# A hybrid decoder step on one core: row maxima turned by one matmul per group onto up to four rows of the query operand

## The chip, the cores and the metric

The kernel runs on one core of one Trainium2 chip. The metric is the device time of one execution in microseconds. A core has a matrix engine (TensorE; PE in the profile, PEld for its weight loads), VectorE (DVE), ScalarE (ACT), GpSimd (POOL) and SyncE (SP), which here issues most DMAs. Each engine runs its own queue of instructions in order and waits on semaphores that the others count up. A matmul writes to one of 8 PSUM banks; all other tiles lie in SBUF, in 128 partitions.

## What is computed

One inference step of a decoder trunk with a short-convolution layer and a forgetting-attention layer, for a prompt of 1040 tokens (1024 and 16 learned ones) and for 32 sample tokens over a paged cache. Only the attention of the prompt heads bears on the change:

```python
def forget_attention(q, k, v, c_q, c_k, q_pos, k_pos):
    s = jnp.einsum('nqhd,nkhd->nhqk', q, k, preferred_element_type=jnp.float32) * (HEAD_DIM ** -0.5)
    s = s + (jnp.transpose(c_q, (0, 2, 1))[:, :, :, None] - jnp.transpose(c_k, (0, 2, 1))[:, :, None, :])
    causal = k_pos[None, :] <= q_pos[:, None]
    s = jnp.where(causal[None, None], s, NEG_INF)
    p = jax.nn.softmax(s, axis=-1)
    return jnp.einsum('nhqk,nkhd->nqhd', p.astype(v.dtype), v)
```

There are 16 heads of 64 values. The softmax needs the largest logit of each query (its row maximum), which is subtracted before the exponential.

## The kernel before

The trunk runs through stages: token loads and norms, convolution mixer, a first MLP, keys and values, queries, the attention of the prompt heads, the output projection together with the sample tokens' attention, a second MLP. The change lies in the prompt heads, some 271 us of the 2548.5, and in head 0's maxima, which are found among the query units ahead of them.

**Operands.** For head h the query operand QA (`q_hi_ext` in the trace) and the key operand CK (`k_hi_ext`) are [128, 1040] tiles, in three sets that take turns (SETS). Rows 0 to 63 hold the head's values, rows 64 (HD) and on hold extra terms of the dot product: 1 in QA against c in CK (rows 65 and 66), and in row 64 the maximum of the query with a minus in QA against 1 in CK. While the maxima are found, row 64 of QA holds zeros, put there by a DMA of `load_head` (L1576), which is issued up to two heads ahead. Logits come out keys by queries, so the maximum of a query has to lie along a row of QA.

**Maxima of the next head.** While head h is weighed, `max_logits` and `reduce_max` run for head h + 1, in sixteen uses u (USES) of a ring of two banks (RING): TensorE writes logits, queries by keys, VectorE reduces them. The maxima of a tile of 128 queries come out as a column of `NMR` (`row_max`). They are turned in three groups (SHIFTS): A is tiles 0 to 3 (16, 128, 128 and 128 queries), B tiles 4 to 6, C tiles 7 and 8. Per group TensorE multiplies each column with the identity (L1109), one matmul with a single column of weights per tile, side by side into one bank row; ScalarE copies that row with scale -1 into row 64 of QA (`keep_shift`, L1161) and counts `nm_kept` up. Before a bank is used again, `ring_wait` waits for its reduction or for `nm_kept`; the banks of A (u = 9), B (u = 11), C (u = 15) and then u = 1 of the next head follow each other in the same bank.

**The order of the loop.** A head is split into 8 groups g of pairs of key tile and query chunk, t = 8h + g. TensorE runs `logits(t + 2)`, then `weigh_values(t)` with the uses of the next head between its matmuls: A at g = 4, B at g = 5, C at g = 0 of its own head. ScalarE runs `exp_logits(t)`, which are two exponentials (L1214 in full precision, L1219 rounded, which counts `h_done`) and for g = 7 two small ones more (L1216, L1221); then `keep_shift` for A behind g = 5, for B behind g = 6, for C behind g = 1; then `keep_chunk` (L1292), a copy of the weighed values, for the group before last or the one before that. VectorE forms the low part of the probabilities (`probs_lo`, L1231) from both exponentials. The logits have two pairs of banks, so `logits(t + 2)` waits for `h_done` of t. The logits of the next head's first group are called logits(8) below, of its second logits(9), counted on from the head in hand; they wait for group 6 and group 7.

```python
                for i in SHIFTS[x]:
                    q, rows = max_rows(i)
                    mm = pe.matmul(PS[0:1, bank, q - first:q - first + rows], NMR[:, hh, i:i + 1], IDR[:, 0:rows],
                                   start=True, stop=True)
...
            act.activation(QA[h % SETS][HD:HD + 1, q0:q1], PS[0:1, bank_of(h, u), 0:q1 - q0], ACT.Copy, scale=-1.0)\
               .then_inc(nm_kept, 1)
```

Of the kernel before, what the change touches and what calls it, by code (L numbers as in the profile page):

```python
# [23 lines left out]
F32 = mybir.dt.float32  # L24
# [3 lines left out]
ACT = mybir.ActivationFunctionType  # L28
# [175 lines left out]
RING = 2  # L204
HI_RING = 3
SETS = 3


def max_rows(i):

    return (0, TAIL) if i == 0 else (TAIL + P * (i - 1), P)
# [8 lines left out]
def trunk(nc, a, out):  # L220

    ctx = ExitStack()
    with ctx:
# [852 lines left out]
        def bank_of(h, u):  # L1076

            return (4 if h else 6) + u % RING

        def reds_through(h, u):  # L1080

            return N_RED * h + sum(REDS[:u + 1])

        def ring_wait(h, u):

            h0, u0 = (h, u - RING) if u >= RING else (h - 1, u - RING + NUSE)
            if h0 < 0:
                return
            if USES[u0] in SHIFTS:
                pe.wait_ge(nm_kept, N_SH * h0 + "ABC".index(USES[u0]) + 1)  # L1090
            else:
                pe.wait_ge(red_done, reds_through(h0, u0))

        def max_logits(h, u):

            _, hh = head(h)
            x, bank = USES[u], bank_of(h, u)
            qa, ck = QA[h % SETS], CK[h % SETS]
            if u == 0:
                pe.wait_ge(h_loaded[h % SETS], 64 * (h // SETS + 1))  # L1100
            ring_wait(h, u)
            if u == NORM_USE + RING and NORM_HEAD < h <= NORM_HEAD + G:
                pe.wait_ge(aux_read, AX_Q + 3 * (KC - 1) + h - NORM_HEAD)
            if x in SHIFTS:
                pe.wait_ge(nm_ready, N_SH * h + "ABC".index(x) + 1)
                first = max_rows(SHIFTS[x][0])[0]
                for i in SHIFTS[x]:
                    q, rows = max_rows(i)
                    mm = pe.matmul(PS[0:1, bank, q - first:q - first + rows], NMR[:, hh, i:i + 1], IDR[:, 0:rows],  # L1109
                                   start=True, stop=True)  # L1110
            elif x == "M":
                for j, i in enumerate(FIRST_KEYS):
                    q, rows = max_rows(i)
                    pe.matmul(PS[:, bank, TAIL * j:TAIL * (j + 1)], qa[:, q:q + rows], ck[:, 0:TAIL],
                              start=True, stop=True)
                to = PS[0:TAIL, bank, P:P + TAIL]
                pe.matmul(to, qa[:, 0:TAIL], ck[:, 0:TAIL], start=True, stop=False)
                mm = pe.matmul(to, IDR[:, 0:TAIL], MASK[:, 0:TAIL], start=False, stop=True)
            else:
                i, a, b = x  # L1120
                q, rows = max_rows(i)
                mm = pe.matmul(PS[:, bank, 0:b - a], qa[:, q:q + rows], ck[:, a:b], start=True, stop=True)  # L1122
            mm.then_inc(mx_done, 1)
# [32 lines left out]
        def keep_shift(h, x):  # L1156

            u = USES.index(x)
            q0, q1 = max_rows(SHIFTS[x][0])[0], sum(max_rows(SHIFTS[x][-1]))
            act.wait_ge(mx_done, NUSE * h + u + 1)  # L1160
            act.activation(QA[h % SETS][HD:HD + 1, q0:q1], PS[0:1, bank_of(h, u), 0:q1 - q0], ACT.Copy, scale=-1.0)\  # L1161
               .then_inc(nm_kept, 1)

        def ops_done(t):

# [6 lines left out]
        def logits(t):  # L1172

            h, g = divmod(t, NG)
            if h == HEADS:
                return
            _, hh = head(h)
            qa, ck = QA[h % SETS], CK[h % SETS]
            if g == 0:
                pe.wait_ge(x_loaded[hh], 64 * (h // 2 + 1))  # L1180
            if g == 0 or CHUNK_OF[g] != CHUNK_OF[g - 1]:
                pe.wait_ge(nm_kept, N_SH * h + CHUNK_OF[g] + 1)
            ge(pe, h_done, ops_done(t - 2))
            for c, j, q0, w, keys, bank, col in GROUPS[g]:
                diagonal, paired = q0 == P * j, (g, j) in PAIRED or (g, j + 1) in PAIRED
                b, k = 2 * (t % 2) + bank, slice(P * j, P * j + keys)
                mm = pe.matmul(PS[0:keys, b, col:col + w], ck[:, k], qa[:, q0:q0 + w], start=(g, j) not in PAIRED,  # L1187
                               stop=False)
                mm = pe.matmul(PS[0:keys, b, col:col + w], DK[hh][:, k], QB[hh][:, q0:q0 + w], start=False,  # L1189
                               stop=not diagonal)  # L1190
                if (g, j) in PAIRED:
                    to = PS[:, b, 0:2 * PAIRED[g, j]].rearrange("p (a k) -> p a k", a=2)[:, :, 0:P]
                    mm = pe.matmul(to, MASK[:, :], twice(IDR[:, :]), start=False, stop=True)
                elif diagonal and not paired:
                    mm = pe.matmul(PS[0:keys, b, col:col + keys], MASK[:, 0:keys], IDR[:, 0:keys], start=False,
                                   stop=True)
            mm.then_inc(st_done, 1)
# [359 lines left out]
        def attention_loaders(stage_out):  # L1557
# [11 lines left out]
            def load_head(h):  # L1569

                n, rows = h % SETS, slice(HD * h, HD * h + HD)
                ge(sp, st_done, NG * (h - SETS + 1))
                for to, src in ((QA[n][OWN], qh_rows), (CK[n][OWN], kh_rows)):
                    sp.dma_start(to.bitcast(F32), src[rows]).then_inc(h_loaded[n], 16)
                sp.dma_start(CK[n][HD + 1:HD + 3].bitcast(F32), c_rows[h]).then_inc(h_loaded[n], 16)
                sp.dma_start(QA[n][HD:HD + 1].bitcast(F32), CK[n][HD + 3:HD + 4].bitcast(F32)).then_inc(h_loaded[n], 16)  # L1576

            def load_cross(h):

# [105 lines left out]
        def extend(n):  # L1685

            pool.memset(CK[n][EXT].bitcast(F32), 0.0).then_inc(ext_ready, 1)
            pool.wait_ge(ext_ready, 4 * n + 1)
            pool.memset(QA[n][EXT].bitcast(F32), 0.0).then_inc(ext_ready, 1)
            pool.wait_ge(ext_ready, 4 * n + 2)  # L1690
            pool.memset(CK[n][HD:HD + 1].bitcast(F32), 1.0).then_inc(ext_ready, 1)
            pool.wait_ge(ext_ready, 4 * n + 3)
            pool.memset(QA[n][HD:HD + 3].bitcast(F32), 1.0).then_inc(ext_ready, 1)
            pool.wait_ge(ext_ready, 4 * n + 4)
# [341 lines left out]
        def attention_tensor():  # L2036
            first_max(KC - 1)
            pe.wait_ge(unit_read, U_O)
            logits(1)
            pe.wait_ge(nm_kept, N_SH)  # L2040
            for t in range(NG * HEADS):
                h, g = divmod(t, NG)
                if h == HEADS - 1 and g in (2, 4):
                    past_turn(g - 2)
                    past_turn(g - 1)
                if t == 5:
                    pe.wait_ge(v_zero, 8)
                logits(t + 2)
                weigh_values(t, uses_of(h, g))


            for u in range(KC):
                unit(U_O + u, hi=HH, lo=HL, ready=o_ready if u == 0 else None,
                     mid={k: decode_step(KC * u + k) for k in range(KC)}, groups=(0, 1), bank=lambda s, g: 2 * s + g)
# [21 lines left out]
        def past_turn(g):  # L2076

            if g == 0:
                pe.wait_ge(lp_loaded, 16 * DB * NPAGE)
                pe.wait_ge(red_done, N_RED * HEADS)  # L2080
                pe.wait_ge(nm_kept, N_SH * HEADS)
            ge(pe, past_kept, g - 1)
            for x in range(4):
                mm = pe.transpose(PS[0:NH, 4 + g % 2, P * x:P * x + P], LPG[:, 4 * g + x], ident[:, :])
            mm.then_inc(past_done, 1)
# [1064 lines left out]
        def _(tensor):  # L3150
# [182 lines left out]
            for n in range(1, KC - 1):  # L3333
                sums, mid = head_sums(U_Q, n % 2, ax(AX_Q + 3 * n, 0, 0), KC + n), {}
                for k in range(len(FIRST_USES[n])):
                    def first(n=n, k=k):
                        first_max(n, k)
                    mid[2 + k] = first

                def norm(n=n, f=sums[6]):  # L3340
                    if FIRST_USES[n]:
                        pe.wait_ge(red_done, reds_through(0, FIRST_USES[n][-1]))
                        pe.wait_ge(nm_kept, sum(USES[u] in SHIFTS for u in range(FIRST_USES[n][-1] + 1)))
                    f()

                def end(n=n, f=sums[7]):
                    f()
                    if n == KC - 2:
                        first_logits()
                unit(U_Q + n + 1, mid={**mid, 6: norm, 7: end})  # L3350
# [30 lines left out]
```

## Time and profile before

| | us |
|---|---|
| median of 3 runs | 2550.76 (2548.99 to 2550.79) |
| the profiled execution's own time | 2550.68 |
| its span, first to last instruction | 2548.5 |
| TensorE busy (PE) | 2518.2, 99% |
| VectorE busy | 1819.5, 71% |
| ScalarE busy | 1050.1, 41% |

"Busy" is the time in which an engine had an instruction of its own in execution; the span's own shares are means over stages that differ. The granted TensorE clock is full through the stage of the heads. In the timelines a row gives the start in us from the span's start, the duration in us, engine, line of the code, operation, output<-input, shapes and how many instructions in a row were put together; behind it in brackets the time that the engine stood idle before and what ended it. A matmul's duration counts until its last result is written, so consecutive ones overlap; how fast they follow each other is read from their starts. In the grouped rows "a, b" is the busy time in us and the mean of one in ns.

### The profile page before, as it was taken

What the parts mean: (1) busy time and instruction counts of PE and PEld (TensorE: products, weight loads), DVE (VectorE), ACT (ScalarE), POOL (GpSimd) and SP (SyncE); (2) the same over time, 40 slices, a digit from 0 to 9 for tenths busy, and PEclk for the clock granted to TensorE, in tenths of its full rate; (3) what the DMA queues carried; (4) which work ended last, traced back from release to release, by engine and by line L of the source; (5) the groups of instructions that cost most, each with busy time, mean ns of one, the idle gap of its engine ahead of it and who ended that gap; (6) DMA issues with size and microseconds to landing.
All of it is one profiled execution on the core that took longest, in us unless ns stands there. A gap on an engine that the chain in (4) does not pass through costs nothing.

```text
span 2548.5 us, 45902 instructions
## 1 busy us (share of the span) xinstructions
PE 2518.2 (99%) x18300; PEld 2468.4 (97%) x18300; DVE 1819.5 (71%) x2462; ACT 1050.1 (41%) x1510; POOL 23.9 (1%) x48
## 2 busy tenths in 40 slices
PE   8999999999999999999999999999999999999998
PEld 8999999999999999999999999988899999999998
DVE  6434437666688998954345898877696666899986
ACT  4111124333333323365245777765553333333233
POOL 0000000000000000000000100000000000000000
PEclk9999999999999999999999999999999999999999
DMA  4111111333353322025424566634323333533112
GB/s 126 45 41 49 41 43 43 121 101 101 101 199 102 124 72 79 16 85 161 118 70 144 139 145 168 148 120 151 97 84 101 101 101 102 186 136 124 63 52 69
DMA packets 249038, 259.42 MB, mean 102 GB/s; under 512 B 18144, under 2 KB 184192, under 8 KB 248898
## 3 DMA queue, kind: packets, MB, share of 16 engines
q1 hardware_dynamic: 229638, 248.37, 31.3%
q10 hardware_dynamic: 19260, 9.09, 1.3%
q8 instruction: 99, 1.62, 0.3%
q14 instruction: 41, 0.34, 0.0%
HBM read 193.86 MB, written 63.42 MB: 101 GB/s over the span
## 4 chain that ended last, share of the span: by engine, by line
PE 92%; DVE 3%; ACT 2%; issue 1%; ACTq 0%; DMA 0%; SPq 0%; DVEq 0%
PE ps L596 28%; PE ps L808 25%; PE ps L863 24%; PE ps L828 2%; PE ps L1272 2%; PE ps L1122 1%; PE ps L1187 1%; PE ps L1273 1%; PE ps L1274 1%; PE ps L1189 1%; PE ps L710 1%; PE ps L647 1%; PE ps L1320 0%; DVE w_lo L580 0%; PE ps L1109 0%
## 5 line engine op out<-in xcount | busy, mean ns | idle before, releaser
L863 PE MATMUL ps<-h_op,w_op 128*128 128x268 f32 x4912 | 614.2, 286 | 0.2
L863 PEld LDWEIGHTS ps<-h_op,w_op 128*128 128x128 f32 x4912 | 609.5, 188 | 0.7 <-DVE w_op L903 0.6
L596 PE MATMUL ps<-x_hi,w_hi 128*128 128x358 f32 x1248 | 279.8, 330 | 2.8 <-DVE w_lo L580 1.6
L596 PE MATMUL ps<-x_hi,w_lo 128*128 128x358 f32 x1248 | 275.5, 327 | 0.0
L596 PE MATMUL ps<-x_lo,w_hi 128*128 128x358 f32 x1248 | 275.0, 326 | 0.0
L580 DVE TENSOR_TENSOR w_lo<-w_raw,w_hi 128x1024 fp32r<-128x1024 f32 x76 | 92.9, 1222 | 250.9 <-ACT w_hi L572 250.9
L874 ACT ACTIVATE w_op<-w_op_f 128x2048 fp32r<-128x2048 f32 (+1 forms) x54 | 97.6, 1808 | 381.9 <-PE ps L863 361.5
L596 PEld LDWEIGHTS ps<-x_hi,w_hi 128*128 128x128 f32 x1248 | 213.4, 189 | 6.6 <-DVE w_lo L580 2.4
L596 PEld LDWEIGHTS ps<-x_lo,w_hi 128*128 128x128 f32 x1248 | 215.8, 189 | 0.0
L596 PEld LDWEIGHTS ps<-x_hi,w_lo 128*128 128x128 f32 x1248 | 215.6, 189 | 0.0
L1060 DVE TENSOR_TENSOR t<-ps,t 128x536 f32<-128x536 f32 x180 | 128.8, 715 | 120.1 <-PE ps L808 111.3
L572 ACT ACTIVATE w_hi<-w_raw 128x1024 fp32r<-128x1024 f32 x76 | 80.1, 1055 | 287.8 <-PE ps L596 283.5
L991 DVE TENSOR_TENSOR acc<-ps,acc 128x536 f32<-128x536 f32 x256 | 174.4, 708 | 14.3 <-PE ps L863 13.9
L903 DVE TENSOR_TENSOR h_op<-h_op_f,h_op 128x2144 fp32r<-128x2144 f32 (+1 forms) x56 | 125.9, 2248 | 42.4 <-ACT h_op L874 42.4
L808 PE MATMUL ps<-x_hi,a_lo 128*128 128x268 f32 x720 | 148.3, 287 | 0.0
L808 PE MATMUL ps<-x_T_hi,s_lo 128*128 128x268 f32 x720 | 147.7, 286 | 0.0
L1028 ACT ACTIVATE t<-t 128x536 f32<-128x536 f32 x90 | 58.8, 653 | 182.6 <-DVE t L1034 182.6
L903 DVE TENSOR_TENSOR w_op<-w_op_f,w_op 128x2048 fp32r<-128x2048 f32 (+1 forms) x54 | 115.7, 2143 | 0.0
L1231 DVE TENSOR_TENSOR probs_lo<-probs_f,probs_hi 128x768 fp32r<-128x768 f32 (+3 forms) x128 | 98.5, 769 | 23.5 <-ACT probs_hi L1219 9.5
L808 PEld LDWEIGHTS ps<-x_hi,a_lo 128*128 128x128 f32 x720 | 112.9, 189 | 0.0
L808 PEld LDWEIGHTS ps<-x_T_hi,s_lo 128*128 128x128 f32 x720 | 112.5, 188 | 0.0
L874 ACT ACTIVATE h_op<-h_op_f 128x2144 fp32r<-128x2144 f32 (+1 forms) x56 | 104.5, 1870 | 8.3 <-DVE h_op_f L951 8.3
(368 smaller groups left out, 5180.0 us busy)
## 6 DMA issues: line engine op xcount, KB each, us to landing
raw_a<-in_mlp_w SPq DMA_DIRECT2D x120, 256.0 KB, 3.1
h_op_f<-h_rows SPq DMA_DIRECT2D x24, 1072.0 KB, 6.5
w_op_f<-in_mlp_w SPq DMA_DIRECT2D x24, 1024.0 KB, 7.4
h_rows<-t SPq DMA_DIRECT2D x90, 268.0 KB, 2.1
w_raw<-in_conv_w_in SPq DMA_DIRECT2D x24, 512.0 KB, 3.8
w_raw<-in_w_kv SPq DMA_DIRECT2D x16, 512.0 KB, 4.8
w_raw<-in_w_o SPq DMA_DIRECT2D x16, 512.0 KB, 3.8
k_page<-in_cache_k SPq DMA_DIRECT2D x16, 512.0 KB, 4.4
```

Source lines behind the costliest of these rows:

```text
L572: act.activation(WH[:, s], RAW[:, s], ACT.Copy).then_inc(w_hi, 1)
L580: dve.tensor_tensor(WL[:, s], RAW[:, s], WH[:, s].bitcast(F32), ALU.subtract).then_inc(w_lo, 1)
L596: mm = pe.matmul(PS[:, bank(s, g), 0:GW], w[:, s, k], x[:, k, g * GW:(g + 1) * GW], start=(k == 0 and n == 0), stop=(k == KC - 1 and n == 2))
L808: mm = pe.matmul(PS[:, 2 * p + g, 0:QW], w[:, k], x[:, k, g * QW:(g + 1) * QW], start=(k == 0 and j == 0), stop=(k == KC // 2 - 1 and j == 2))
L828: mm = pe.matmul(PS[:, 2 * p + g, 0:QW], w[:, k, P * m:P * m + P], x[:, k, a:a + QW], start=(k == 0 and j == 0), stop=(k == UNIT_TILES - 1 ...
L863: mm = pe.matmul(PS[:, 2 * p + g, 0:QW], w[:, k, P * m:P * m + P], x[:, k, QW * g:QW * g + QW], start=(k == 0 and j == 0), stop=(k == tile ...
L874: act.activation(h_flat(to, n), h_flat(raw, n), ACT.Copy).then_inc(second_hi, 1)
L903: dve.tensor_tensor(h_flat(pieces[1], n), h_flat(raw, n), h_flat(pieces[0], n).bitcast(F32), ALU.subtract) .then_inc(second_lo, 1)
L991: mm = dve.tensor_tensor(two(to), pair(PAIRS2[l][i]), two(to), ALU.add)
L1028: act.activation(UB[USLOT[q]], UB[USLOT[q]], ACT.Square).then_inc(hf_done, 1)
L1060: dve.tensor_tensor(two(to), pair(p), two(other), ALU.add).then_inc(m_read, 1)
L1231: dve.tensor_tensor(PBL[:, t % HI_RING, 0:nb * w], PF[:, t % 2, 0:nb * w], PBH[:, t % HI_RING, 0:nb * w].bitcast(F32), ALU.subtract).then_ ...
```

## The change

Each group of maxima is turned by one matmul. Its weights are the 4, 3 or 2 columns of `NMR` at once, and its moving operand is the whole identity, so row k of the output holds the maxima of the group's tile k. These up to four rows have to land in QA so that each query meets just its own tile's. For each tile j of the group one copy writes n rows of QA, 96 to 96 + n - 1 (MAX_ROW), over that tile's queries, with a scale per row that is read from column j of the identity: 1 for row j and 0 for the others. The keys hold -1 in rows 96 to 99, and row 64 of CK stays zero. The DMA that lays in zeros for a head covers four rows instead of one. `nm_kept` counts 9 copies a head instead of 3, and each wait on it is put to the count at the end of the same group.

```diff
+MAX_ROW = 96
...
+        def shifts_kept(h, x):
+
+            return NT * h + sum(len(SHIFTS[y]) for y in "ABC"[:x + 1])
+
...
-                pe.wait_ge(nm_kept, N_SH * h0 + "ABC".index(USES[u0]) + 1)
+                pe.wait_ge(nm_kept, shifts_kept(h0, "ABC".index(USES[u0])))
...
-                first = max_rows(SHIFTS[x][0])[0]
-                for i in SHIFTS[x]:
-                    q, rows = max_rows(i)
-                    mm = pe.matmul(PS[0:1, bank, q - first:q - first + rows], NMR[:, hh, i:i + 1], IDR[:, 0:rows],
-                                   start=True, stop=True)
+                i0, n = SHIFTS[x][0], len(SHIFTS[x])
+                mm = pe.matmul(PS[0:n, bank, 0:P], NMR[:, hh, i0:i0 + n], IDR[:, :], start=True, stop=True)
...
-            q0, q1 = max_rows(SHIFTS[x][0])[0], sum(max_rows(SHIFTS[x][-1]))
+            n = len(SHIFTS[x])
             act.wait_ge(mx_done, NUSE * h + u + 1)
-            act.activation(QA[h % SETS][HD:HD + 1, q0:q1], PS[0:1, bank_of(h, u), 0:q1 - q0], ACT.Copy, scale=-1.0)\
-               .then_inc(nm_kept, 1)
+            for j, i in enumerate(SHIFTS[x]):
+                q, rows = max_rows(i)
+                act.activation(QA[h % SETS][MAX_ROW:MAX_ROW + n, q:q + rows], PS[0:n, bank_of(h, u), 0:rows],
+                               ACT.Copy, scale=ident[0:n, j:j + 1]).then_inc(nm_kept, 1)
...
-                pe.wait_ge(nm_kept, N_SH * h + CHUNK_OF[g] + 1)
+                pe.wait_ge(nm_kept, shifts_kept(h, CHUNK_OF[g]))
...
-                sp.dma_start(QA[n][HD:HD + 1].bitcast(F32), CK[n][HD + 3:HD + 4].bitcast(F32)).then_inc(h_loaded[n], 16)
+                sp.dma_start(QA[n][MAX_ROW:MAX_ROW + 4].bitcast(F32), CK[n][MAX_ROW + 4:MAX_ROW + 8].bitcast(F32))\
+                  .then_inc(h_loaded[n], 16)
...
-            pool.memset(CK[n][HD:HD + 1].bitcast(F32), 1.0).then_inc(ext_ready, 1)
+            pool.memset(CK[n][MAX_ROW:MAX_ROW + 4].bitcast(F32), -1.0).then_inc(ext_ready, 1)
...
-            pe.wait_ge(nm_kept, N_SH)
+            pe.wait_ge(nm_kept, shifts_kept(0, N_SH - 1))
```

## Rows read from the trace of the kernel before

**Rows 1.** Windows, one head: length, then busy (count) of PE, PEld, DVE, ACT, POOL; clock.
```profile
1543.43:1560.07 16.64, 16.64 (x124) 15.61 (x121) 14.51 (x38) 12.34 (x25) 0.00 (x0) 1.00 0.51 119
```

**Rows 2.** List of waits, 1411 to 1683 us: us in total, times, longest.
```profile
ACT q_hi_ext L1161 <- PE ps L1109: 49.4, 45, 1.9
```

**Rows 3.** Timeline around A in one head, 1543 to 1545.5 us.
```profile
1543.43 0.36 PE L1109 MATMUL ps<-ident,row_max 128*1 128x16 f32 x4
1543.58 0.19 PEld L1187 LDWEIGHTS ps<-q_hi_ext,k_hi_ext 128*128 128x128 f32 x1
1543.83 0.49 ACT L1161 ACTIVATE q_hi_ext<-ps 1x400 fp32r<-1x400 f32 x1 [1.68 <-PE ps L1109]
1544.35 0.62 ACT L1214 ACTIVATE probs_f<-ps 128x544 f32<-128x544 f32 x1
1544.87 0.62 ACT L1219 ACTIVATE probs_hi<-ps 128x544 fp32r<-128x544 f32 x1
```

**Rows 4.** Timeline around B and logits(9) in the same head, 1545.5 to 1548 us.
```profile
1545.58 0.34 PE L1109 MATMUL ps<-ident,row_max 128*1 128x128 f32 x3
1545.70 0.19 PEld L1187 LDWEIGHTS ps<-q_hi_ext,k_hi_ext 128*128 128x128 f32 x1
1545.95 0.48 ACT L1161 ACTIVATE q_hi_ext<-ps 1x384 fp32r<-1x384 f32 x1 [0.46 <-PE ps L1109]
1546.46 0.49 ACT L1292 ACTIVATE o_and_sums<-ps 128x384 f32<-128x384 f32 x1
1547.70 0.16 ACT L1221 ACTIVATE tail_hi<-ps 16x16 fp32r<-16x16 f32 x1
1547.95 0.59 DVE L1231 TENSOR_TENSOR probs_lo<-probs_f,probs_hi 128x416 fp32r<-128x416 f32 x1 [1.04 <-ACT tail_f L1216]
1547.97 0.19 PEld L1187 LDWEIGHTS ps<-q_hi_ext,k_hi_ext 128*128 128x128 f32 x1
```

**Rows 5.** Timeline, logits(9)'s weights at the first and the last of 15 heads.
```profile
1429.34 0.16 ACT L1221 ACTIVATE tail_hi<-ps 16x16 fp32r<-16x16 f32 x1
1429.61 0.19 PEld L1187 LDWEIGHTS ps<-q_hi_ext,k_hi_ext 128*128 128x128 f32 x1
...
1664.83 0.16 ACT L1221 ACTIVATE tail_hi<-ps 16x16 fp32r<-16x16 f32 x1
1665.10 0.19 PEld L1187 LDWEIGHTS ps<-q_hi_ext,k_hi_ext 128*128 128x128 f32 x1
```

**Rows 6.** Timeline around C in the same head as rows 3.
```profile
1551.53 0.28 PE L1109 MATMUL ps<-ident,row_max 128*1 128x128 f32 x2
1551.59 0.19 PEld L1272 LDWEIGHTS ps<-probs_hi,v_hi 128*128 128x128 f32 x1
1551.84 0.37 ACT L1161 ACTIVATE q_hi_ext<-ps 1x256 fp32r<-1x256 f32 x1 [1.21 <-PE ps L1109]
...
1552.55 0.19 PEld L1122 LDWEIGHTS ps<-k_hi_ext,q_hi_ext 128*128 128x128 f32 x1
...
1553.22 0.82 ACT L1219 ACTIVATE probs_hi<-ps 128x768 fp32r<-128x768 f32 x1
1554.31 0.94 DVE L1231 TENSOR_TENSOR probs_lo<-probs_f,probs_hi 128x768 fp32r<-128x768 f32 x1
```

**Rows 7.** Groups by line and shape, ACT, whole span.
```profile
L1161 ACT ACTIVATE q_hi_ext<-ps 1x384 fp32r<-1x384 f32 x16 | 7.7, 480 | 8.9 <-PE ps L1109 8.9
L1161 ACT ACTIVATE q_hi_ext<-ps 1x256 fp32r<-1x256 f32 x16 | 6.0, 372 | 18.4 <-PE ps L1109 18.4
L2469 ACT ACTIVATE x_T_hi<-x_T_f,vectors 128x536 fp32r<-128x536 f32 x8 | 5.2, 727 | 0.0
L2476 ACT ACTIVATE x_T_hi<-x_T_f 128x536 fp32r<-128x536 f32 x8 | 4.5, 636 | 0.0
```

**Rows 8.** Timeline, four copies with a scale from a tile, 410 to 424 us.
```profile
413.66 2.62 ACT L2469 ACTIVATE x_T_hi<-x_T_f,vectors 128x536 fp32r<-128x536 f32 x4
```

**Rows 9.** Timeline, logits of head 0 behind its C, 1414.7 to 1415.6 us.
```profile
1414.96 0.19 PEld L1187 LDWEIGHTS ps<-q_hi_ext,k_hi_ext 128*128 128x128 f32 x1 [0.48 <-ACT q_hi_ext L1161]
```

More of the change, by code:

```diff
@@ L2080, in past_turn @@
                 pe.wait_ge(red_done, N_RED * HEADS)
-                pe.wait_ge(nm_kept, N_SH * HEADS)
+                pe.wait_ge(nm_kept, shifts_kept(HEADS - 1, N_SH - 1))
             ge(pe, past_kept, g - 1)
@@ L3342, in norm @@
                         pe.wait_ge(red_done, reds_through(0, FIRST_USES[n][-1]))
-                        pe.wait_ge(nm_kept, sum(USES[u] in SHIFTS for u in range(FIRST_USES[n][-1] + 1)))
+                        pe.wait_ge(nm_kept, sum(len(SHIFTS[USES[u]]) for u in range(FIRST_USES[n][-1] + 1) if USES[u] in SHIFTS))
                     f()
```

## The prediction

> **What bounds the kernel now.** I read first the busy table of one head in the stage that the change touches: TensorE is busy for all of the head's 16.64 us, ScalarE for 12.34, at a full granted clock [rows 1]. So TensorE sets the pace, and what TensorE is spared is worth its full length, as long as no order from another engine comes later than it does now. ScalarE looks idle for a quarter of the head. The list of waits says how it is idle: the copies of the maxima (L1161) are waited for with ScalarE standing at them, 49.4 us over the stage in 45 waits [rows 2]. ScalarE runs its queue in order, so these pauses are not slack; what stands behind a copy starts when the copy is over.
>
> The third reading, the timeline around the copies, is the one that decides. Times below count from the first of A's matmuls, 1543.43. TensorE turns A at 0; ScalarE starts the copy at 0.40, then the two exponentials of group 6, at 0.92 and 1.44, over at 2.06 [rows 3]. TensorE turns B at 2.15 and loads the weights of logits(8) at 2.27. That load needs the exponentials of group 6 (h_done). ScalarE takes the copy of B at 2.52, keep_chunk at 3.03, then group 7, whose last exponential ends at 4.43; TensorE loads the weights of logits(9), which waits for exactly that one, at 4.54, 0.11 after it [rows 4]. The same 0.11 stands between these two instructions at the first and at the last of the 15 heads that have A and B in this stage [rows 5], and at all of those between. So TensorE takes its order from ScalarE there in every head already. The list of waits hides it, since the array is still draining its last matmul meanwhile.
>
> **TensorE's part of the change.** Each group's matmuls go from 4, 3 and 2 to one. The next weight load can start when the last matmul of the group has started: 0.15 after the first of A's four [rows 3], 0.12 for B's three [rows 4], 0.06 for C's two [rows 6]. With one matmul it starts with it. That spares 0.15 + 0.12 + 0.06 = 0.33 us a head, 16 x 0.33 = 5.3 us in all. A weight load of 4 columns in place of 1 lies under the matmul before it, as that of 1 does. This is the whole gain on offer.
>
> **ScalarE's part.** One copy becomes 4, 3 or 2, each with a scale read from a tile. A copy of 256 columns takes 372 ns, one of 384 takes 480: 0.84 ns a column, so one of 128 with a constant takes 372 - 128 x 0.84 = 264 ns and one of 16 takes 264 - 112 x 0.84 = 170. What a scale from a tile costs shows in the same shape with and without it: 727 against 636 ns, 91 ns more [rows 7]. So 355 ns for a tile of 128 and 260 for the 16 rows of tile 0. Four copies of that kind, one behind the other, take 2.62 us where 4 x 0.727 is 2.91: each starts 0.10 before the one before it ends [rows 8]. But today's single copy doesn't overlap what follows: it ends at 0.89 and the exponential starts at 0.92 [rows 3]; the same 0.03 of air follows B [rows 4]. Whether copies from partition 0 to partition 96 overlap each other is not in this trace. Bounds: 0.10 of overlap at each step, or 0.03 of air. I take the overlap inside a group and the air behind its last one, as neighbours of one kind are likeliest to run like rows 8, and the step to another kind like rows 3.
> The Trainium skill (ScalarE: Activation LUTs, What ACT_TABLE_LOAD costs) speaks against the change too: an operand that is a pointer adds about 93 ns to an ACTIVATE. Its base of 186 ns is above the 157 that rows 7 leave for these copies (264 - 107). By its figures the 128-column copy would take some 386 ns, and the same sum as below would come to an estimated +0.60 a head, near 2560.
>
> **The sum for a head.** (1) A: one matmul ends at 0.22 instead of 0.36, so the copies start at 0.26 instead of 0.40. They take 0.16 + 2 x 0.255 + 0.355 + 0.03 = 1.055, where the single one took 0.52. Group 6 starts at 1.315 instead of 0.92 and ends at 2.455 instead of 2.06. (2) The load for logits(8) could start at 2.27 - 0.27 = 2.00; its order comes at 2.455 + 0.11 = 2.565. TensorE stands there for 0.56 us: a new wait, and the 0.27 spared is gone with 0.30 more. (3) B's matmul is out at 2.00, so ScalarE no longer waits for it; the copies of B start at 2.485, take 2 x 0.255 + 0.355 + 0.03 = 0.895, and keep_chunk starts at 3.38 instead of 3.03. (4) From there to the load for logits(9) nothing changes, so it comes 0.35 late, at 4.89. TensorE itself would be there at 2.565 + 2.27 = 4.84 at the latest, so ScalarE decides. The head has lost 0.35 us up to here. B's matmul writes into the bank of the ring that held A and waits for A's last copy; that is over at 1.285, long before 2.00.
> (5) C: TensorE is spared 0.06. From C's matmul (1551.53) the copies start at 0.26, take 0.255 + 0.355 + 0.03 = 0.64, and keep_chunk starts at 0.90 where it is 0.31 + 0.37 + 0.03 = 0.71 now; the exponentials of the head's group 2 end at 2.51 + 0.19 = 2.70 [rows 6]. VectorE needs them for the subtraction that it starts at 2.78 now, and could start 0.09 after them, its lag behind a last exponential [rows 4]. That makes 2.79, where VectorE without this would be at 2.72: the 0.06 is used up and C comes out at nothing. The weight load that waits for C's copies in the ring (u = 1, now at 1.02 and then at 0.96) gets its order at 0.87 + 0.11 = 0.98, no loss to speak of.
> (6) Behind C both of ScalarE's delays end: it stands 1.68 us at A and 1.21 us at C in this head [rows 3, 6], so nothing is carried into the next. The calm between makes the loss per head a constant and not one that grows.
> (7) Head 0 has A and B among the query units, where ScalarE isn't pressed: 0.27 gained. C of head 0 is waited for by TensorE directly, 0.48 us now [rows 9]; its copies end 0.61 instead of 0.37 after they start, 0.24 lost. Together nothing.
> Sum: 15 x 0.35 = 5.3 us. The profiled execution took 2550.68 us (span 2548.5 and 2.2 around it), as good as the median of 2550.76. Forecast: 2550.7 + 5.3 = **2556.0 us**.
>
> **What costs nothing.** The zero row that is laid in anew for each head becomes four rows, by one DMA issue as before, and a head ahead of its use; the memset of -1 is one for one, three times in all and long before; the counts in the waits change with the number of copies, not their places. If the DMA's cover went, its price would be its landing, but a head, 16.64 us [rows 1], lies between the issue and the use.
>
> **Rivals.** (a) *The copies don't overlap*: slower still. Then A takes 0.29 + 3 x 0.385 = 1.445 and group 6 starts at 1.705; B starts at 2.875 and takes 1.155, so keep_chunk is at 4.03, 1.0 late; C takes 0.77, 0.37 more than now, starts 0.05 earlier and so is 0.32 late, of which the 0.18 between 2.51 + 0.09 and 2.78 covers a part: 0.14 lost. 1.14 x 15 = 17 us, 2568. For it: today's copy overlaps nothing before or after it. Against: rows 8. (b) *The air isn't there*: the last copy of a group overlaps its follower like any other instruction, 0.13 less for A and B each. Then A and B take 0.925 + 0.765 = 1.69. The load for logits(9) comes at its old time when the two together take 1.60 (3.03 less the 0.26 before them, the 1.14 of group 6 and 0.03 of air), so 0.09 a head is lost there, C keeps its 0.06, and 15 x 0.03 = 0.5 us: 2551.2. That is not slower, by one mechanism at one place, and 1.60 us is the point from which it decides. (c) *The whole gain comes*: if the scale from a tile is free on one to four partitions and all copies overlap, A takes 0.07 + 3 x 0.164 = 0.56 and B 0.49, together 1.05. The whole 0.27 is kept below 1.60 - 0.27 = 1.33. Then 5.3 us are gained: 2545.4. Against it stand the 91 ns of rows 7; for it only that no row shows this scale on so few partitions. (d) That the change doesn't spare the matmuls' time is excluded by rows 3, 4 and 6, which show each one's share.
>
> **How the numbers follow.** The forecast case with its neighbours (2553 to 2560): 0.50. Case (a) and what lies between, 2560 to 2568: 0.23. Case (b), 2548 to 2553: 0.18. Case (c): 0.06. Something else, 0.03. The range leaves out (c) and the last end of (a): 2549 to 2567. A measurement of this kernel can tell about 0.2%, 5.1 us, from no change. The forecast lies at that edge: slower by more takes six tenths of its case, (a) and half of the rest, 0.55; within takes four tenths of it and (b), 0.39; faster has (c), 0.06.
>
> **What would show it.** TensorE: one matmul per group, and the next weight load with it. ScalarE: copies of 0.26 and 0.355 us, starts 0.255 apart, 0.03 of air behind the last; waiting at A 1.5 to 1.8 us as before, at B none where it is 0.46 now. TensorE: the load for logits(8) 0.11 behind group 6's last exponential, which it isn't yet, with about 0.5 us of visible waiting; the load for logits(9) still 0.11 behind its own; 0.35 us more between one head's A and the next. The prediction is wrong at step 1 if the copies are of another length or spacing, at step 2 if TensorE doesn't stand there, and at step 6 if ScalarE hasn't caught up at C.

## Result and profile after

| | before | after |
|---|---|---|
| median of 20 runs each, same chip | 2550.88 (2548.99 to 2553.54) | 2555.85 (2554.41 to 2558.19) |
| ratio, 95% interval | | 1.0020 [1.0013, 1.0026] |
| the profiled execution's own time, its span | 2550.68, 2548.5 | 2555.05, 2552.9 |

The change makes the kernel 5.0 us slower; the forecast was 5.3. The page of after, its busy table and the head of its chain:

```profile
PE 2517.4 (99%) x18204; PEld 2463.2 (96%) x18204; DVE 1820.1 (71%) x2462; ACT 1068.0 (42%) x1606; POOL 24.3 (1%) x48
PE 90%; ACT 4%; DVE 4%; issue 1%; DMA 0%; ACTq 0%; SPq 0%; DVEq 0%
```

ScalarE has 96 instructions more (6 x 16 heads) and 18 us more of work. TensorE is busy for no longer than before, but ScalarE's part of the chain that ends last has grown from 2% to 4%. Shares don't say where. The timeline of a head does. It answers to [rows 3, 4] and shows, out of after's window 1546.5 to 1552.5 us, ScalarE's rows around the copies and the loads and matmuls that bear on them:

```profile
1546.76 0.22 PE L1112 MATMUL ps<-ident,row_max 128*4 128x128 f32 x1
1546.76 0.19 PEld L1191 LDWEIGHTS ps<-q_hi_ext,k_hi_ext 128*128 128x128 f32 x1
...
1547.02 1.01 ACT L1165 ACTIVATE q_hi_ext<-ps,ident 4x16 fp32r<-4x16 f32 x4 [1.54 <-PE ps L1112]
1547.03 0.72 DVE L1235 TENSOR_TENSOR probs_lo<-probs_f,probs_hi 128x544 fp32r<-128x544 f32 x1
...
1547.81 0.19 PEld L1276 LDWEIGHTS ps<-probs_hi,v_hi 128*128 128x128 f32 x1 [0.22 <-DVE probs_lo L1235]
...
1548.05 0.63 ACT L1218 ACTIVATE probs_f<-ps 128x544 f32<-128x544 f32 x1
...
1548.58 0.62 ACT L1223 ACTIVATE probs_hi<-ps 128x544 fp32r<-128x544 f32 x1
...
1548.90 0.22 PE L1112 MATMUL ps<-ident,row_max 128*3 128x128 f32 x1
1549.22 0.86 ACT L1165 ACTIVATE q_hi_ext<-ps,ident 3x128 fp32r<-3x128 f32 x3
...
1549.31 0.19 PEld L1191 LDWEIGHTS ps<-q_hi_ext,k_hi_ext 128*128 128x128 f32 x1 [0.45 <-issue]
1549.34 0.41 PE L1191 MATMUL ps<-q_hi_ext,k_hi_ext 128*128 128x384 f32 x1 [0.22 <-ACT probs_hi L1223]
...
1550.10 0.49 ACT L1296 ACTIVATE o_and_sums<-ps 128x384 f32<-128x384 f32 x1
...
1550.49 0.51 ACT L1218 ACTIVATE probs_f<-ps 128x416 f32<-128x416 f32 x1
...
1551.35 0.16 ACT L1225 ACTIVATE tail_hi<-ps 16x16 fp32r<-16x16 f32 x1
...
1551.62 0.19 PEld L1191 LDWEIGHTS ps<-q_hi_ext,k_hi_ext 128*128 128x128 f32 x1 [0.16 <-issue]
```

From A's matmul at 1546.76: the four copies start at 0.26 and take 1.01; group 6's last exponential ends at 2.44, and the weights of logits(8) are loaded at 2.55, 0.11 behind it, after standing 0.45 us. B's copies start as soon as the exponential is over; ScalarE no longer waits for B. The weights of logits(9) come at 4.86, where before had them at 4.54 [rows 4]. The list of waits over the stage, 1430 to 1672 us (total, times, longest), has the new wait in its second row:

```profile
ACT q_hi_ext L1165 <- PE ps L1112: 36.7, 28, 1.6
PEld ps L1191 <- issue: 8.1, 25, 0.5
PEld ps L1276 <- DVE probs_lo L1235: 7.3, 28, 0.4
PE ps L1191 <- ACT probs_hi L1223: 3.2, 14, 0.2
```

Before has no such wait of TensorE's at L1187 in that stretch. Of these four rows it has only the first and the third:

```profile
ACT q_hi_ext L1161 <- PE ps L1109: 47.1, 43, 1.7
...
PEld ps L1272 <- DVE probs_lo L1231: 3.7, 13, 0.4
```

From the first of the 15 heads' logits(9) to the last, a head takes 17.162 us after and 16.821 before: 0.341 more, 5.1 us over 15. That is as much as the medians differ by. It isn't the same in every head: 0.37 over the first seven of these 14 steps, where VectorE does norms as well, and 0.31 over the last seven.

### The profile page after: what moved, and what is told of

It reads as the page before. It is cut to its first block, busy times and chain, and to the rows that moved or that the text cites. A ratio compares the mean times of both kernels' runs of the same rounds, so it can differ in the third digit from the quotient of the medians.

```text
span 2552.9 us, 45806 instructions
## 1 busy us (share of the span) xinstructions
PE 2517.4 (99%) x18204; PEld 2463.2 (96%) x18204; DVE 1820.1 (71%) x2462; ACT 1068.0 (42%) x1606; POOL 24.3 (1%) x48
## 4 chain that ended last, share of the span: by engine, by line
PE 90%; ACT 4%; DVE 4%; issue 1%; DMA 0%; ACTq 0%; SPq 0%; DVEq 0%
PE ps L597 28%; PE ps L809 25%; PE ps L864 24%; PE ps L829 2%; PE ps L1191 1%; PE ps L1276 1%; PE ps L1124 1%; PE ps L1277 1%; PE ps L1278 1%; PE ps L1193 1%; ACT q_hi_ext L1165 1%; PE ps L648 1%; PE ps L711 1%; ACT probs_f L1218 1%; ACT probs_hi L1223 0%
```

## Experiments

All tables below use two measures: "a head", the mean of the 14 steps from the first logits(9) to the last, and the stretches of the last 8 heads, in which ScalarE and VectorE carry nothing but the attention: from A's matmul to B's, on to the first matmul of logits(9), to C's, to the next A's. Both are read from one trace per kernel; the medians are those of all its executions.

### The price of the split and of the scale

Two kernels take the change apart. In the first the copies stay nine, with a scale read from the identity, but the old matmuls with one column each are back, so every copy takes a single row:

```diff
-                i0, n = SHIFTS[x][0], len(SHIFTS[x])
-                mm = pe.matmul(PS[0:n, bank, 0:P], NMR[:, hh, i0:i0 + n], IDR[:, :], start=True, stop=True)
+                first = max_rows(SHIFTS[x][0])[0]
+                for i in SHIFTS[x]:
+                    q, rows = max_rows(i)
+                    mm = pe.matmul(PS[0:1, bank, q - first:q - first + rows], NMR[:, hh, i:i + 1], IDR[:, 0:rows],
+                                   start=True, stop=True)
...
-                act.activation(QA[h % SETS][MAX_ROW:MAX_ROW + n, q:q + rows], PS[0:n, bank_of(h, u), 0:rows],
-                               ACT.Copy, scale=ident[0:n, j:j + 1]).then_inc(nm_kept, 1)
+                act.activation(QA[h % SETS][MAX_ROW:MAX_ROW + 1, q:q + rows],
+                               PS[0:1, bank_of(h, u), q - first:q - first + rows], ACT.Copy,
+                               scale=ident[0:1, 0:1]).then_inc(nm_kept, 1)
```

> Undo TensorE's part of the change alone: 9 matmuls a head with one column of weights, as before, into one row; 9 copies of one row, each with a scale from a tile, as many and as long as in the changed kernel. Nothing is left out. My theory: TensorE's share of the gain is lost against waits in any case; one matmul for A only lets the copies start 0.14 earlier. So 0.50 a head more than the kernel before instead of 0.34: near 2558.7. Rival: the merged matmuls earn their full 0.33 a head on TensorE and something else costs 0.67: then this one comes to 2561.

The second is the same with a constant:

```diff
-                               scale=ident[0:1, 0:1]).then_inc(nm_kept, 1)
+                               scale=1.0).then_inc(nm_kept, 1)
```

> The same with a constant as the scale: 9 matmuls and 9 copies of one row a head, no scale from a tile. My theory: a 128-column copy takes 0.264 us and starts 0.164 after the one before it, A takes 0.69 instead of 1.03 and B 0.62 instead of 0.88, so 0.11 a head over the kernel before: near 2552.5. Rival: the number of copies is what costs, not the operand from a tile: as old_turn, near 2558.7.

| | median, us | ratio [95%] | a head, us |
|---|---|---|---|
| before | 2550.85 | | 16.821 |
| split, constant scale | 2551.91 | 1.0006 [0.9998, 1.0015] | 16.943 |
| split, scale from a tile | 2560.05 | 1.0033 [1.0020, 1.0046] | 17.365 |
| after | 2555.85 | 1.0020 [1.0013, 1.0026] | 17.162 |

Read down the last column: three, two and one more instructions a head cost 0.12, reading their scale from a tile costs 0.42, and the merged matmuls give back 0.20 of it. The constant came out as expected (0.12 a head, 0.11 forecast). With the scale from a tile a head is 0.54 longer than before, nearer to the theory's 0.50 than to the rival's 0.67; its median lies between the two. The groups by line and shape show why (us busy, mean ns of one): first the constant, then the pointer on one row, then after with up to four rows.

```profile
L1168 ACT ACTIVATE q_hi_ext<-ps 1x128 fp32r<-1x128 f32 x128 | 25.1, 253 | 25.2 <-PE ps L1114 25.2
L1168 ACT ACTIVATE q_hi_ext<-ps 1x16 fp32r<-1x16 f32 x16 | 2.8, 172 | 24.2 <-PE ps L1114 24.2
```

```profile
L1168 ACT ACTIVATE q_hi_ext<-ps,ident 1x128 fp32r<-1x128 f32 x128 | 36.9, 346 | 20.7 <-PE ps L1114 20.3
```

```profile
L1165 ACT ACTIVATE q_hi_ext<-ps,ident 3x128 fp32r<-3x128 f32 x48 | 13.7, 347 | 1.7 <-PE ps L1112 1.4
L1165 ACT ACTIVATE q_hi_ext<-ps,ident 4x16 fp32r<-4x16 f32 x16 | 4.2, 263 | 21.9 <-PE ps L1112 21.8
```

346 - 253 = 93 ns for the scale read from a tile (the pointer), 263 - 172 = 91 at 16 columns, and nothing for more rows. Seven copies at A and B with 93 ns each are 0.65 a head. With the constant ScalarE still waits 0.29 for B in the timeline; that slack is used up first, and the 0.36 left are about what is added between B and logits(9) in the last 8 heads (2.532 to 2.908); 0.04 more lie behind C. The merged matmuls' 0.20 comes through ScalarE: the copies of A start 0.26 behind A's first matmul instead of 0.40, and 0.154 are missing between B and logits(9) in the last 8 heads; the other 0.06 is C's.

### The groups apart

In one kernel only C is in the new form, matmul and copies, in the other only A and B. The other groups stay on row 64, so both rows 64 and 96 to 99 get their zeros, by one more DMA a head. For C alone (the other kernel has the two conditions the other way round, and both have the like at the copies):

```diff
-                for i in SHIFTS[x]:
+                if x == "C":
+                    i0, n = SHIFTS[x][0], len(SHIFTS[x])
+                    mm = pe.matmul(PS[0:n, bank, 0:P], NMR[:, hh, i0:i0 + n], IDR[:, :], start=True, stop=True)
+                for i in SHIFTS[x] if x != "C" else ():
```

> The change for C alone, A and B as before, with the zero row and the four zero rows laid in by two DMAs a head. Nothing is left out. My theory: C spares TensorE 0.06 us and loses it again to VectorE's wait for the exponentials of group 2; the DMA is hidden: no change, 2550.9. Rival: C or the DMA carries a part of the loss: up to 2 us more.

> The change for the groups A and B alone, C as before: one matmul and 4 and 3 copies for A and B, into rows 96 to 99; C two matmuls and one copy into row 64; keys' rows 1 and -1, both laid in zero rows (one more DMA a head). Nothing is left out. My theory: the whole loss of 0.34 a head lies here, 15 x 0.34 = 5.1 us: near 2556. Rival: C has a part in it, then less.

| last 8 heads, us | A to B | to logits(9) | to C | to the next A | sum | median, ratio [95%] |
|---|---|---|---|---|---|---|
| before | 2.134 | 2.431 | 3.527 | 8.659 | 16.751 | |
| C alone | 2.134 | 2.434 | 3.526 | 8.638 | 16.730 | 2551.03, 1.0003 [0.9994, 1.0012] |
| A and B alone | 2.129 | 2.754 | 3.530 | 8.662 | 17.075 | 2556.14, 1.0023 [1.0013, 1.0033] |
| after | 2.132 | 2.755 | 3.530 | 8.635 | 17.052 | 2555.85, 1.0020 [1.0013, 1.0026] |

The loss sits in one of the four stretches, between B and logits(9), and belongs to A and B. C gives 0.02 where 0 was forecast.

The medians of these two kernels hold something more, and the expectation that the added DMA is hidden was wrong. In both traces TensorE stands at the first use of head 1, ahead of the stretches in the table, until that DMA has landed, 1.41 us with C alone and 1.37 with A and B alone:

```profile
1419.56 0.30 PEld L1123 LDWEIGHTS ps<-k_hi_ext,q_hi_ext 128*128 128x128 f32 x2 [1.41 <-DMA q_hi_ext<-k_hi_ext]
```

Neither before nor after has such a wait. So these two medians can't say within 1.4 us what a group costs; the stretches can.

### The order of ScalarE's queue

If the loss is that logits(8) and logits(9) wait behind copies that nobody needs yet, it must go when the copies are put one group of exponentials later, with all their work unchanged:

```diff
-SHIFT_AT = {4: "A", 5: "B"}
+SHIFT_AT = {5: "A", 6: "B"}
```

It is applied to after, and to before as well, since the 0.11 in [rows 4, 5] says that before takes its order from ScalarE too.

> The changed kernel with ScalarE's queue in another order: the copies of A behind the exponentials of group 6 instead of group 5, those of B behind group 7 instead of 6. Nothing is left out. My theory: the change loses because nine copies stand in ScalarE's queue ahead of the exponentials for which the weight loads of logits(8) and logits(9) wait. With the copies behind them A's last copy is over about 1.9 us after A's matmul and B's about 3.8, both just before TensorE asks for them (2.0 and 4.1), and the loads of logits(8) and logits(9) wait for nothing: 0.2 us a head less than in the kernel before, and 0.06 to 0.1 at C: near 2546.5 us. Rival: the cost is the copies' or the four rows' own (ring of banks, VectorE, DMA), wherever they stand: it stays near 2556.

> The kernel before with the same other order of ScalarE's queue, matmuls and copies as they were. My theory: in every head the load of logits(9) is some 0.09 us late against the end of the matmul ahead of it, and C another 0.05; both go: 15 x 0.12 = 1.8 us, near 2549.1. Rival: that order came late for nothing (the array was busy), 2550.9.

| | median, us | ratio to before [95%] | A to B | to logits(9) | to C | to the next A | sum |
|---|---|---|---|---|---|---|---|
| before, later copies | 2547.28 | 0.9985 [0.9976, 0.9994] | 2.126 | 2.433 | 3.317 | 8.662 | 16.538 |
| after, later copies | 2545.99 | 0.9980 [0.9971, 0.9989] | 2.125 | 2.316 | 3.320 | 8.633 | 16.394 |

The loss is gone with the same copies: 9.9 us less than after, and 4.9 less than before. The timeline of after with later copies:

```profile
1544.49 0.22 PE L1112 MATMUL ps<-ident,row_max 128*3 128x128 f32 x1
1544.49 0.19 PEld L1191 LDWEIGHTS ps<-q_hi_ext,k_hi_ext 128*128 128x128 f32 x1
...
1545.12 0.16 ACT L1225 ACTIVATE tail_hi<-ps 16x16 fp32r<-16x16 f32 x1
...
1545.31 0.86 ACT L1165 ACTIVATE q_hi_ext<-ps,ident 3x128 fp32r<-3x128 f32 x3
...
1546.57 0.19 PEld L1191 LDWEIGHTS ps<-q_hi_ext,k_hi_ext 128*128 128x128 f32 x1
```

Group 7's last exponential is over at 1545.28, and logits(9)'s weights follow at 1546.57, 1.29 us later, where it was 0.11 in both kernels. Logits(8) is loaded in the moment B's matmul starts, with no bracket behind it. ScalarE's list of waits over 1430 to 1672 us has kept the wait at C and lost the one at A:

```profile
ACT q_hi_ext L1165 <- PE ps L1112: 17.0, 15, 1.2
```

The old form won more than expected, 3.6 us instead of 1.8. Its 0.21 a head doesn't lie where the late load is (2.433, as before) but behind it, from logits(9) to C. In that stretch probs_lo(7) stands 1.04 in before [rows 4] and not at all once the copies are later, and VectorE's reductions behind it are earlier. The starts of the matmuls divide it. Behind logits(9)'s late load the second matmul follows 0.25 behind the first instead of 0.17. First before, then before with the later copies:

```profile
1548.01 0.41 PE L1187 MATMUL ps<-q_hi_ext,k_hi_ext 128*128 128x384 f32 x1
1548.26 0.34 PE L1189 MATMUL ps<-q_lo_hi,k_hi_lo 128*128 128x384 f32 x1
```

```profile
1547.52 0.34 PE L1187 MATMUL ps<-q_hi_ext,k_hi_ext 128*128 128x384 f32 x1
1547.69 0.34 PE L1189 MATMUL ps<-q_lo_hi,k_hi_lo 128*128 128x384 f32 x1
```

That is 0.08 over the last 8 heads, close to the 0.09 expected. Another 0.11 comes at the load of use 14 (1549.16), which in before stands 0.05 behind the end of VectorE's reduction of the bank:

```profile
1549.04 0.07 DVE L1145 DVE_READ_ACCUMULATOR2_ANT max_parts<- 128x1 f32 x1
...
1549.16 0.19 PEld L1122 LDWEIGHTS ps<-k_hi_ext,q_hi_ext 128*128 128x128 f32 x1
```

With the later copies the reduction is in time. The last 0.03 lies right in front of C.

### The work beside it: the values' low part

Between A and B the merged matmul gained nothing: 2.132 instead of an expected 1.99. In the timeline of after above, weigh_values(5) loads at 1547.81, right behind probs_lo(5), and that is 1.05 behind A's matmul in both kernels. VectorE makes `v_lo` (values_lo of the next head) just ahead of probs_lo(5). So it was moved two groups on, to behind probs_lo(6) and ahead of probs_lo(7):

```diff
-                    if g == 3:
+                    if g == 5:
                         values_lo(h + 1)
```

It was tried on after, on after with the later copies, and on before with the later copies.

> The changed kernel with values_lo moved in the same way. My theory: the wait at weigh_values(5) goes, but the loads of logits(8) and logits(9) wait for ScalarE's copies and exponentials, which start from A's matmul and not from group 5's weighing: TensorE stands 0.15 us longer there, and the time stays at 2555.9. Rival: VectorE's wait is a part of the change's loss: 2 us less.

> order_after with VectorE's values_lo moved from behind the reductions of group 3 to behind those of group 5. Nothing is left out. In the trace after, the 0.15 us that A's one matmul spares is gone 0.3 us later already: weigh_values(5) waits for probs_lo(5), and that stands in VectorE's queue behind values_lo. My theory: with values_lo later, TensorE gets there 0.15 us earlier in each of 15 heads and nothing else is late: 2.2 us under order_after, near 2543.8. Rival: the queue of VectorE is full anyway, the wait comes back at weigh_values(7) or at C: 2546.

> The kernel before with both moves, ScalarE's copies behind the exponentials of groups 6 and 7 and values_lo behind group 5, and with its own 9 matmuls and 3 copies a head. Nothing is left out. Together with v_late_order (2542.71 us) it prices the merged matmuls by themselves, where neither ScalarE nor VectorE holds TensorE up around A and B. My theory: TensorE reaches weigh_values(5) in the old form just when probs_lo(5) is over, so moving values_lo gives nothing here: as order_before, near 2547.3, and the matmuls are worth 0.3 us a head, 4.6 us. Rival: the two moves give the old form the same 3.3 us as the new one (order_after to v_late_order): 2544.0, and the merged matmuls are worth only the 1.3 us that lay between order_before and order_after.

| values_lo moved, and | median, us | ratio to before [95%] | A to B | to logits(9) | to C | to the next A | sum |
|---|---|---|---|---|---|---|---|
| after | 2558.89 | 1.0033 [1.0020, 1.0045] | 1.851 | 3.041 | 3.531 | 8.633 | 17.056 |
| after, later copies | 2542.71 | 0.9969 [0.9957, 0.9981] | 1.849 | 2.349 | 3.337 | 8.643 | 16.178 |
| before, later copies | 2545.20 | 0.9979 [0.9970, 0.9988] | 1.995 | 2.428 | 3.316 | 8.668 | 16.407 |

The first row is the clearest picture of the case. Between A and B 0.28 is gained, and all of it is lost again in front of logits(9), because ScalarE's queue gives that order and hasn't become earlier; the sum stays at 17.056 against 17.052. The kernel is 3.0 us slower all the same, which was not expected. That lies in the early heads, where VectorE also does the query norms: over the first seven steps a head takes 17.86 us against 17.28 of after, over the last seven 17.04 in both. VectorE's timeline there:

```profile
1446.50 0.75 DVE L1258 TENSOR_TENSOR v_lo<-v_raw,v_hi 128x576 fp32r<-128x576 f32 x1
1447.16 1.27 DVE L3017 TENSOR_TENSOR squares_r<-squares,t_r 128x1074 fp32r<-128x1074 f32 x1
1448.35 0.58 DVE L1235 TENSOR_TENSOR probs_lo<-probs_f,probs_hi 128x416 fp32r<-128x416 f32 x1
1448.85 0.15 DVE L1238 TENSOR_TENSOR tail_lo<-tail_f,tail_hi 16x16 fp32r<-16x16 f32 x1
```

v_lo and the squares of a norm now stand together in front of probs_lo(7) and tail_lo, and the list of waits (1430 to 1672 us) has TensorE waiting for the latter, 4.9 us where after has 0.5, and longer at the logits than the 8.1 of after:

```profile
PEld ps L1191 <- issue: 12.5, 27, 0.7
...
PEld ps L1276 <- DVE tail_lo L1238: 4.9, 6, 0.9
```

The third row shows an expectation that failed: the old form was held between A and B as well, by 0.13 (2.126 to 1.995), which no wait in its list shows. The timeline of before does show it. The load for weigh_values(5) follows the end of probs_lo(5) by 0.05, and by the same 0.05 in all 15 heads:

```profile
1543.71 0.72 DVE L1231 TENSOR_TENSOR probs_lo<-probs_f,probs_hi 128x544 fp32r<-128x544 f32 x1
...
1544.48 0.19 PEld L1272 LDWEIGHTS ps<-probs_hi,v_hi 128*128 128x128 f32 x1
```

For the same reason the second row lies 3.3 us under after with the later copies, where 2.2 were expected. With these two orders out of the way, the merged matmuls can be read nearly by themselves, third row against second: 0.146 at A, 0.08 up to logits(9), 0.02 back up to C, 0.025 behind C, together 0.23 in the last 8 heads and 2.5 us in the medians.

Nearly, because a third order stands in the new form. Up to the load of logits(8) it is 0.26 ahead of the old one. Then use 13 writes into the bank that held B and waits for B's last copy, which now ends later (1543.36 + 0.86 = 1544.22). In after with the later copies and values_lo moved:

```profile
1543.36 0.86 ACT L1165 ACTIVATE q_hi_ext<-ps,ident 3x128 fp32r<-3x128 f32 x3
...
1544.10 0.19 PEld L1278 LDWEIGHTS ps<-probs_lo,v_hi 128*128 128x128 f32 x1
...
1544.27 0.19 PEld L1124 LDWEIGHTS ps<-k_hi_ext,q_hi_ext 128*128 128x128 f32 x1
```

The load at 1544.27 stands 0.05 behind that copy in 14 of 15 heads, and in all but one of them 0.15 to 0.19 behind the load before it, where the old form has 0.13. It takes the lead from 0.25 to 0.21.

The second row, 8.1 us faster than before, is the best version found: the new matmuls, the copies one group later, and values_lo at g = 5.

## Why the prediction was right, and where not

By the steps of its sum, in us from A's matmul unless another start is named:

| step | predicted | measured |
|---|---|---|
| 1, A's copies start; take, with the air behind them | 0.26; 1.055 | 0.26; 1.03 |
| 1, group 6 over | 2.455 | 2.44 |
| 2, B's matmul | 2.00 | 2.14 |
| 2, load of logits(8) | 2.565 | 2.55 |
| 3, B's copies take; keep_chunk starts | 0.895; 3.38 | 0.88; 3.34 |
| 4, load of logits(9), before 4.54 | 4.89 | 4.86 |
| 5, from C's matmul: group 2 over; VectorE's probs_lo behind it | 2.70; 2.79 | 2.70; 2.78 |
| 5, C's matmul to the next A's, against before | 0 | -0.02 |
| 6, ScalarE stands at A; at C | 1.5 to 1.8; no number | 1.54; 1.16 |
| 7, exponential behind head 0's C, against before | 0.24 late | 0.24 late |
| loss a head | 0.35 | 0.341 |
| all | 2556.0 | 2555.85 |

**Right.** ScalarE's queue gives the order for logits(8) and logits(9), and the copies stand in front of it: shown by the later copies, which take the whole loss away and leave the work as it is. The load of logits(8) lies 0.11 to 0.12 behind group 6's last exponential, that of logits(9) 0.11 behind group 7's, in all 15 heads. The price of the scale from a tile, worked out at 91 ns from [rows 7], is 93. The Trainium skill (ScalarE: Activation LUTs, What ACT_TABLE_LOAD costs) puts an operand that is a pointer at about 93 ns, and the trace agrees; its base of 186 ns does not fit these copies, since 253 - 107 (128 columns of 0.84) leaves 146.

The choice in step 1, overlap inside a group and air (a short pause) behind it, was right too. C's two copies in after, and those of A and B above, show it:

```profile
1555.17 0.22 PE L1112 MATMUL ps<-ident,row_max 128*2 128x128 f32 x1
1555.43 0.60 ACT L1165 ACTIVATE q_hi_ext<-ps,ident 2x128 fp32r<-2x128 f32 x2 [1.16 <-PE ps L1112]
```

Two copies of 0.348 take 0.60, so they overlap by 0.10; the next instruction starts 0.02 to 0.03 behind the last one's end. That puts an end to rival (a), in which each copy has air around it. Rival (b), no air, would need A and B to take 1.69 together; they take 1.91 with their air. Rival (c), a free scale, falls with the 93 ns.

The reason given for that choice, "the step to another kind", doesn't hold, so the value came out right in part by luck. keep_chunk's copy and the exponential behind it are of different kinds and overlap by 0.10 (after, 1550.10 and 1550.49 above). In every trace looked at (before, after, after with the later copies) the pause stands only where ScalarE goes from rows 0 on of its output to row 64 or 96, or back. That it is the start row that makes the pause is argued from this; no run moved it.

**Close in the sum, less so by head.** The last 8 heads lose 0.30 (16.751 to 17.052), less than the forecast 0.35, since logits(9) is 0.32 late and C gives 0.02. The early ones lose more, 0.37 over the first seven steps, because the stretch from logits(9) to C grows as well where VectorE does norms. The prediction had no such term. The two misses cancel in part, so 0.341 against 0.35 is better than the model was.

**Wrong, step 2.** B's matmul was to be out at 2.00, earlier by A's 0.15. It is out at 2.14. The prediction looked for what TensorE waits on at logits(8), and took the stretch up to B as TensorE's own. But weigh_values(5) stands in it and waits for probs_lo(5), behind v_lo on VectorE: 1.05 behind A's matmul in both kernels. So A's 0.15 is lost there already, and TensorE stands 0.41 at logits(8) and not 0.56. It made no difference to the time because logits(8) has a later order anyway; moving v_lo gave 0.28 back at this place and nothing in the sum. The sign was there: weigh_values(5) is loaded 0.05 behind probs_lo(5) in every head of before, as logits(9) is 0.11 behind ScalarE. In rival (c) it would have counted, since that one keeps A's 0.15.

**Wrong without effect: the DMA's cover.** That a head, 16.64 us, lies between the issue of the zero row and its use doesn't hold for head 1. Before issues its zero row at 1414.47 and loads the first use at 1418.02, 3.5 us later; after issues at 1414.90 and loads at 1418.72. That was enough for one DMA, of one row or four, and not for the second one of the kernels with the groups apart.

**A gain only in part.** "The whole gain on offer", 0.33 a head, was read from the distances of starts. For A and B that reading was right: with the other orders out of the way TensorE is 0.26 ahead at logits(8), where 0.27 was forecast. But 0.04 of it is lost again at use 13 behind B's last copy, and of C's 0.06 hardly anything is left, since VectorE's wait for group 2 takes it, as step 5 said. What remains is 0.23, and with v_lo in its old place 0.14 (16.538 to 16.394), as A's 0.146 is then lost at weigh_values(5).

**Not quite the same 5 us.** The single traces differ by 4.4 us in span. After is 0.74 late before A of head 0 is reached, ahead of anything the change touches; 0.27 of that comes back at head 0's A and B, as forecast; 5.3 are lost from head 0's C to the last logits(9); and some 1.4 are given back behind the heads. There TensorE runs for a few us at a granted clock of 0.5, which is its lower level of 1.2 GHz. In before, the 4 us ahead of it and a part of it:

```profile
1678.30:1682.30 4.00, 2.50 (x21) 2.27 (x20) 2.19 (x4) 4.00 (x12) 0.00 (x0) 1.00 0.00 0
...
1684.00:1688.00 4.00, 4.00 (x17) 3.92 (x15) 3.69 (x10) 1.12 (x5) 0.00 (x0) 0.50 0.34 100
```

It lasts 6.8 us in before, right behind the heads, and ahead of it TensorE was busy for 2.50 of 4.00 us. After has the same lull there, 2.50 of 4.00 us in 1684 to 1688, and keeps its clock; its stretch comes 104 us further on and lasts 3.4 us. Four of the other kernels have one of 3.4 us inside head 0, ahead of the heads that the tables measure. One of 3.4 us costs some 1.4 us: from head 0's C to the next A before with the later copies takes 14.25 us, and before 12.82. How often each kernel has one isn't known, with one trace per kernel.

## What to carry over

An engine that waits in its list isn't idle when its queue is in order: ask of each instruction that gets longer what stands behind it in the same queue, and who takes an order from that. Look for a constant lag between one engine's end and another's start, at every place where one engine waits for another and not only at the one under study: 0.11 us at logits(9) and 0.05 at weigh_values(5), in all 15 heads and with no wait in the list. It marks the queue that decides before any wait shows. Where a change moves work onto such a queue, change the place of the work with it: the same copies cost 5 us in front of the exponentials, and behind them the change is worth 1.3 us, or 2.5 with values_lo moved.

## What the runs showed of the hardware

- ScalarE copies from PSUM to SBUF of one row take 172 ns for 16 columns and 253 for 128 with a constant scale, 263 and 346 with a scale read from SBUF. With the scale from SBUF, one row or up to four makes no difference (346, and 341 to 348).
- These copies overlap each other by 0.09 to 0.10 us, and so do a copy and an exponential (0.10) that both write from row 0 on. Between one that writes from row 0 on and one that writes into row 64 or 96 on there is 0.02 to 0.03 us of air instead.
- From the end of an exponential to the TensorE weight load that it releases there are 0.11 us, to VectorE's instruction 0.09. From the end of a copy into row 64 or 96 on to the weight load there are 0.05 (head 0's C, before and after), and as much from the end of VectorE's probs_lo.
- A late weight load need not show in the list of waits, which counts only idle time: while the last matmuls drain, the array still looks busy. Twice the list had nothing: 0.08 us a head at logits(9) and 0.13 at weigh_values(5). The constant lag gave the place, and only taking the cause away gave the size.
